# The seams of a four-stage encoder step: what runs at the end of each stage for the next one, and rows of the sample attention every 6 slots

## The chip, the cores and the metric

One core of a Trainium2 chip. The metric is the device time of one execution of the whole kernel in microseconds, here the median of three runs.

## What is computed

One layer of a hybrid encoder on a prompt of 2048 tokens and on 8 sample rows of 16 tokens with 512 cached tokens each, all in float32, d_model 1024:

```python
z = x @ w_in                     # q latent 256 | kv latent 256 | rotary key 32 | pooling 512
q = rms_norm(q_a, g_q) @ w_q_b   # 8 heads x (64 + 32 rotary)
c = rms_norm(c_raw, g_kv); kr = rope(kr_raw)
# prompt: k, v = c @ w_kv_b, softmax over chunks of 64 up to the query's own
# sample: attention in the latent space over cache and new tokens
pool_out = pool_mix(u, windows 2, 4, 8, 16)
mix = concat(attention, pool_out) @ w_o
x1 = layer_norm(ALPHA * x + mix)
x2 = layer_norm(ALPHA * x1 + conv_ffn(x1) + sigmoid(x1 @ w_pg) * (pe @ w_pe))
```

The outputs are x2 for prompt and sample, the latents c, the rotary keys and the states of pooling and convolution.

## The kernel before, in words

Every product of two matrices is made of three matmuls (lines 84 to 86): both operands are split into a high part, rounded to a type that TensorE (PE) takes in one pass, and a low part, the remainder. The high part is written by ScalarE (ACT), the low part by GpSimd (POOL) or VectorE (DVE) as raw minus high. All loads and stores are issued on one queue, SyncE's (SP). Each engine has its program written out in order; semaphores tie them. There are five stages, and at the end of each every engine waits for all others and for the stage's last stores:

- **project** (from 0 to 266.7 us on PE): w_in for 4 chunks of 512 tokens and then for the 128 sample tokens, whose x pieces are loaded and split 512 wide. In the sample's chunk ACT also splits the 8 weight pieces of the next stage (`split_x(HEADS_C, ...)`), between the latents; SP loads them, then stores the pooling state (line 320), the pooled channels (line 284), the latents (line 292) and the rotary key. The third and fourth pool store wait for an earlier one to land. ACT and POOL run the chunks in loops.
- **heads** (282 to 470): PE makes ten idle matmuls (line 1179), then the 8 q units of the sample, then 64 units of six matmuls for the prompt (per chunk 8 of q, 4 of k, 4 of v, in `ORDER`). DVE rotates q units in three operations (lines 998, 1000, 1009), ACT copies the rest (line 883). The 8 rows of the sample attention are spread over these slots: row r starts at slot `ROW_BASE + ROW_PITCH * r` = 5 + 7r, with parts at fixed distances (scores +1, maxima +2, exponents +3, new tokens +4, scaling +4, new low parts +6, transposes +6, values +9, latents +10). `LATENT_AT` is the slot of the latent queries, 2.
- **attend** (475 to 1018): 8 heads, each 4 strips of 512 queries, 320 units of 128 keys. Before a strip's scores its row maxima are found: PE makes the scores once (`peak`, line 1628), DVE reduces them (line 1571), PE turns them into a row (line 1642), ACT writes it into row 96 of the queries (line 1521). PE makes values of unit i - 4 behind the scores of unit i. ACT makes the exponentials (1491) and their high parts (1498), DVE (1600) and POOL (1461) the low parts of even and odd units. When a strip is done ACT copies its sums (`num`, two buffers, line 1541), which go through DRAM twice, and POOL multiplies (line 1441). In the opening DVE clears masks, and row 96 of the keys (1555), and makes the low part of the rotary key's first chunk (1560) ahead of the first maximum. PE starts with 12 idle matmuls (1614). In the last head the first 7 of 18 weight pieces of the next stage and its first tile are split at units given by `MIX_LOW` and `MIX_TILE`, and PE ends with those 7 pieces of tile 0.
- **mix** (1019 to 1463): 17 tiles of 128 tokens: w_o (8 pieces), residual and norm, transposes, w_pe (2 pieces), w_pg (8 pieces, `gates`). At its start pieces 7 to 17, tile 1 and the embeddings are still to be split; a piece waits for its slot in `work`.
- **ffn** (1463 to 3049): not touched.

## Time and profile before

| | us |
|---|---|
| median of 3 runs (3043.7 to 3048.4) | 3046.28 |
| the profiled execution | 3051.59 |
| its span in the profile | 3049.8 |
| PE busy | 2928.4 |
| DVE / ACT / POOL busy | 1632.2 / 1358.0 / 1401.2 |
| share of time that PE's clock was granted in full, as a mean | 0.979 |

"Busy" is the time in which an engine has an instruction running; idle time in front of an instruction is given with what ended it. PEclk is the clock that TensorE was granted, 1.00 being 2.4 GHz and 0.50 being 1.2 GHz; a value between is a mean of the two. Matmuls overlap, so the spacing of their starts is shorter than their duration. Names begin with the stage: pj, hd and sa (sample attention), at, mx, ff; ho is what is handed over between stages.

### The profile page before, as it was taken

Reading aid. Unit: us, or ns where it says so; the run is one execution under the profiler, and the core shown is the slowest. Engines: PE = TensorE matmul, PEld = TensorE weight load, DVE = VectorE, ACT = ScalarE, POOL = GpSimd, SP = SyncE. Lnnn points to the kernel's source line nnn. Section 1 sums busy time; section 2 is a strip of 40 time slices with the busy share of each in tenths; the row PEclk is TensorE's granted clock in tenths of the full one; section 3 lists DMA queues with packets and bytes.
Section 4 is the critical chain, followed back from the end, with each engine's and each line's share of the span. In section 5 each row is a group of like instructions: output and inputs, shape, how many; then the busy total and the mean of one; then the engine's idle time right before and its main releaser. Section 6 shows DMA issues by size and latency. Waiting matters only on the chain.

```text
span 3049.8 us, 43672 instructions
## 1 busy us (share of the span) xinstructions
PE 2928.4 (96%) x15374; PEld 2575.0 (84%) x15374; DVE 1632.2 (54%) x2177; ACT 1358.0 (45%) x2635; POOL 1401.2 (46%) x831
## 2 busy tenths in 40 slices
PE   8996997999999799999999999999999999999997
PEld 6876876777777588888999999999999999999996
DVE  5635787777777444443344343474344447544446
ACT  5343554777777422221434343443333344444443
POOL 5352553676666522222344343574343447544445
PEclk9997997999999899999999999999999999999998
DMA  4226552213223322222421221242121213312221
GB/s 136 87 86 127 164 161 54 42 42 65 42 45 108 117 89 87 89 87 91 174 69 56 68 65 59 92 157 82 49 76 55 69 62 133 123 63 75 76 76 61
DMA packets 161774, 263.67 MB, mean 86 GB/s; under 512 B 48352, under 2 KB 90048, under 8 KB 160288
## 3 DMA queue, kind: packets, MB, share of 16 engines
q1 hardware_dynamic: 161664, 262.27, 28.0%
q8 instruction: 62, 1.02, 0.1%
q14 instruction: 48, 0.39, 0.0%
HBM read 206.34 MB, written 55.88 MB: 86 GB/s over the span
## 4 chain that ended last, share of the span: by engine, by line
PE 51%; DVE 1%; POOL 0%; issue 0%; DVEq 0%; ACTq 0%
PE ff_u L84 11%; PE ff_u L86 11%; PE ff_u L85 11%; PE ff_d L84 5%; PE ff_d L85 5%; PE ff_d L86 5%; DVE ff_y L2552 0%; DVE ff_y L2601 0%; DVE ff_stats L2584 0%; POOL ff_y L2387 0%; POOL ff_rstd L2377 0%; DVEq L2167 0%; DVE ff_mv L2586 0%; DVE ff_neg_mean L2588 0%; POOL ff_offset L2379 0%
## 5 line engine op out<-in xcount | busy, mean ns | idle before, releaser
L2337 POOL TENSOR_TENSOR ff_w_lo<-ho_raw,ff_w_hi 128x1024 fp32r<-128x1024 f32 x99 | 242.6, 2464 | 491.7 <-ACT ff_w_hi L2410 491.7
L2337 POOL TENSOR_TENSOR mx_w_lo<-ho_raw,mx_w_hi 128x1024 fp32r<-128x1024 f32 x97 | 276.0, 2858 | 230.7 <-ACT mx_w_hi L2410 230.7
L2531 DVE SCALAR_TENSOR_TENSOR ff_cv_a<-ff_up_a,ff_taps,ff_cv_a 128x768 f32<-128x768 f32 (+1 forms) x132 | 154.5, 1171 | 347.0 <-ACT ff_cv_a L2459 339.0
L2552 DVE TENSOR_TENSOR ff_y<-ff_y,ff_d 128x512 f32<-128x512 f32 x374 | 239.6, 682 | 146.3 <-PE ff_d L86 146.2
L2531 DVE SCALAR_TENSOR_TENSOR ff_cv_b<-ff_up_b,ff_taps,ff_cv_b 128x768 f32<-128x768 f32 (+1 forms) x132 | 122.7, 930 | 305.4 <-ACT ff_cv_b L2459 296.8
L1461 POOL TENSOR_TENSOR at_p_lo<-at_p,at_p_hi 128x512 fp32r<-128x512 f32 (+2 forms) x160 | 189.7, 1186 | 178.9 <-ACT at_p_hi L1498 177.1
L1600 DVE TENSOR_TENSOR at_p_lo<-at_p,at_p_hi 128x512 fp32r<-128x512 f32 (+1 forms) x160 | 192.3, 1203 | 67.6 <-ACT at_p_hi L1498 67.4
L84 PE MATMUL ff_u<-ho_hi,mx_w_hi 128*128 128x384 f32 (+1 forms) x690 | 224.9, 326 | 0.7 <-ACTq L2403 0.7
L86 PE MATMUL ff_u<-ho_lo,mx_w_hi 128*128 128x384 f32 (+1 forms) x690 | 225.0, 326 | 0.0
L85 PE MATMUL ff_u<-ho_hi,mx_w_lo 128*128 128x384 f32 (+1 forms) x690 | 224.8, 326 | 0.0
L1491 ACT ACTIVATE at_p<-at_s 128x512 f32<-128x512 f32 (+1 forms) x320 | 169.7, 530 | 103.9 <-PE at_s L1664 50.0
L84 PE MATMUL ff_u<-ho_hi,ff_w_hi 128*128 128x384 f32 x630 | 205.1, 326 | 0.0
L86 PE MATMUL ff_u<-ho_lo,ff_w_hi 128*128 128x384 f32 x630 | 205.0, 325 | 0.0
L85 PE MATMUL ff_u<-ho_hi,ff_w_lo 128*128 128x384 f32 x630 | 205.0, 325 | 0.0
L1498 ACT ACTIVATE at_p_hi<-at_p 128x512 fp32r<-128x512 f32 (+1 forms) x320 | 179.2, 560 | 0.0
L2450 ACT ACTIVATE ff_up_b<-ff_u 128x384 f32<-128x384 f32 x110 | 54.0, 491 | 267.6 <-PE ff_u L86 267.6
L84 PE MATMUL ff_d<-ff_w_hi,ff_h_hi 128*128 128x512 f32 x408 | 159.1, 390 | 4.4 <-DVE ff_y L2552 4.4
L2343 POOL TENSOR_TENSOR ff_h_lo<-ff_h,ff_h_hi 128x768 fp32r<-128x768 f32 (+1 forms) x66 | 117.8, 1786 | 91.4 <-ACT ff_h_hi L2470 91.4
L2544 DVE TENSOR_TENSOR ff_h<-ff_cv_a,ff_cv_b 128x768 f32<-128x768 f32 (+1 forms) x66 | 157.6, 2388 | 3.9 <-issue 0.4
L85 PE MATMUL ff_d<-ff_w_hi,ff_h_lo 128*128 128x512 f32 x408 | 159.1, 390 | 0.0
L86 PE MATMUL ff_d<-ff_w_lo,ff_h_hi 128*128 128x512 f32 x408 | 159.0, 390 | 0.0
L2410 ACT ACTIVATE ff_w_hi<-ho_raw 128x1024 fp32r<-128x1024 f32 x99 | 103.4, 1050 | 124.4 <-DMA ho_raw<-in_w_ffn_p 124.4
(471 smaller groups left out, 8858.6 us busy)
## 6 DMA issues: line engine op xcount, KB each, us to landing
ho_raw<-in_w_ffn_p SPq DMA_DIRECT2D x196, 512.0 KB, 3.7
ho_raw<-in_x_t SPq DMA_DIRECT2D x40, 256.0 KB, 3.1
mx_work<-in_w_mix_p SPq DMA_DIRECT2D x18, 512.0 KB, 3.7
ho_raw<-in_x SPq DMA_DIRECT2D x17, 512.0 KB, 4.1
mx_m_raw<-scratch_mix_t SPq DMA_DIRECT2D x17, 512.0 KB, 4.9
scratch_x_t<-mx_work SPq DMA_DIRECT2D x17, 512.0 KB, 3.2
scratch_y<-mx_work SPq DMA_DIRECT2D x17, 512.0 KB, 3.0
ff_y<-scratch_y SPq DMA_DIRECT2D x17, 512.0 KB, 6.2
```

Source lines behind the costliest of these rows:

```text
L84: pe.matmul(out, lh, rh, start=first, stop=False, **kw)
L85: pe.matmul(out, ll, rh, start=False, stop=False, **kw)
L86: return pe.matmul(out, lh, rl, start=False, stop=last, **kw)
L1461: pool.tensor_tensor(p_lo[:, e % H_RING, 0:b - a], p[:, e % P_RING, 0:b - a], f32(p_hi[:, e % H_RING, 0:b - a]), ALU.subtract).then_inc(lo ...
L1491: act.activation(p[:, i % P_RING, 0:b - a], ps_s[i % S_BANKS][:, 0:b - a], ACT.Exp).then_inc(expd, 1)
L1498: act.activation(p_hi[:, i % H_RING, 0:b - a], p[:, i % P_RING, 0:b - a], ACT.Copy).then_inc(hid, 1)
L1600: dve.tensor_tensor(p_lo[:, e % H_RING, 0:b - a], p[:, e % P_RING, 0:b - a], f32(p_hi[:, e % H_RING, 0:b - a]), ALU.subtract).then_inc(lo_ ...
L2337: pool.tensor_tensor(w_lo[slot], w_raw[n % RAWS].rearrange("p (k c) -> p k c", c=P), f32(w_hi[slot]), ALU.subtract).then_inc(wlo, 1)
L2343: pool.tensor_tensor(h_lo[:, i + extra, 0:w], h[:, i, 0:w], f32(h_hi[:, i + extra, 0:w]), ALU.subtract)\
L2531: op = dve.scalar_tensor_tensor(cv[s][:, 0:pw], up[s][:, k:k + pw], tap, cv[s][:, 0:pw], ALU.mult, ALU.add)
L2544: dve.tensor_tensor(h[:, i, 0:w], cv[0][:, 0:w], cv[1][:, 0:w], ALU.mult).then_inc(mul, 1)
L2552: dve.tensor_tensor(y[:, t, H[i]], y[:, t, H[i]], ps_d[2 * (t % 2) + i][:, :], ALU.add)\
```

## The change

- **project** takes the first pair of x buffers from outside, so that heads finds it filled. x of the sample is loaded and split 128 wide, into the second half of the low and high pair's own rows. Head weights 0 to 3 are loaded before the last chunk's latents are stored and split ahead of the sample's pooling; 4 to 7 are split between the sample's pooling units. The first chunk's q latent and kv latent (4 pieces) are loaded behind the state stores and ahead of the pool stores, and split by ACT and DVE. The late stores of pool and latents get own places and semaphores. The loops of POOL and ACT are written out. PE ends with 20 idle matmuls.
- **heads** starts without idle matmuls with the k units of chunk 0; the 8 sample units go in pairs before slots 2 to 5; row r starts at slot 10 + 6r, the latent queries are at slot 7; PE ends with 14 idle matmuls.
- **attend**: PE starts after one memset with 3 idle matmuls, and its maxima wait only for the masks; the ones in row 96 of the keys and the rotary key's first low part are POOL's; `num` has three buffers; pieces and tile of mix at other units; tile 1 and pieces 7, 8 and 9 are split behind the last unit; PE makes all 8 pieces of tile 0, DVE its residual; SP loads pieces 11 to 14.
- **mix** starts with the statistics of tile 0 on DVE and tile 1 on PE; pieces 10 to 17 are left, 15, 17 and 16 loaded here in this order.

```diff
 def project(nc, g, hand, x_pair):
+            def load_first():
+                for i in range(2):
+                    sp.wait_ge(st_lat[i], nth(CHUNKS - 1, 2, 1) * 16)
+                for k in range(4):
+                    sp.wait_ge(split_lo, x_piece(FIRST_C, k) - RAW + 1)
...
-                    if width == SAMPLE and i >= 2:
-                        sp.wait_ge(st_pool[i % 2], nth(c, 2, 0) * 16)
...
-            load_x(SAMPLE_C)
+            load_x(SAMPLE_C, SAMPLE)
...
             store_pool(last, CW)
+            load_head_weights(range(RAW))
             sp.wait_ge(kr_mul, nth(last, 2, 1))
             load_trig(SAMPLE_C)
             store(last, CW)
-            load_head_weights()
+            load_head_weights(range(RAW, KD))
             sp.wait_ge(evac, nth(SAMPLE_C, 8, 3))
             for grp in range(4):
                 sp.dma_start(g["pool_s"][:, grp], rows32(u[:, grp, 0:ROWS * 32])[:, :, 17:32]).then_inc(st_hist, 16)
+            load_first()
             store_pool(SAMPLE_C, SAMPLE)
...
+            def sample_chunk():
+                split_x(HEADS_C, 1, range(RAW))
+                for i in range(4):
+                    keep_u(SAMPLE_C, i, SAMPLE, True)
+                    if i > 0:
+                        difference(SAMPLE_C, i - 1, SAMPLE)
+                        split_x(HEADS_C, 1, (RAW + i - 1,))
+                difference(SAMPLE_C, 3, SAMPLE)
+                split_x(HEADS_C, 1, (KD - 1,))
+                for i in range(4):
+                    if i == 3:
+                        split_x(FIRST_C, 0, (0, 1))
+                    latent(SAMPLE_C, i, SAMPLE)
+                    pooled(SAMPLE_C, i, SAMPLE)
+                split_x(FIRST_C, 0, (2, 3))
+                roots(SAMPLE_C, SAMPLE)
...
+            for _ in range(PJ_TAIL):
+                pe.matmul(ps[0][:, :], w_hi[:, 0, 0, :], w_hi[:, 0, 0:4, :].rearrange("p a b -> p (a b)"), start=True,
+                          stop=True, skip_group_check=True)
...
-HD_WARM = 10
+PJ_TAIL = 20
+HD_TAIL = 14
-UNITS_H = [(CHUNKS, n) for n in range(HEADS)] + [(c, n) for c in range(CHUNKS) for n in ORDER]
+FIRST_ORDER = (8, 9, 10, 11, 0, 12, 1, 13, 2, 14, 3, 15, 4, 5, 6, 7)
+SAMPLES_BEFORE = {2: (0, 1), 3: (2, 3), 4: (4, 5), 5: (6, 7)}
-ROW_PITCH, ROW_BASE, LATENT_AT = 7, 5, 2
-SPLIT_AT = (3, 5, 7, 9)
+ROW_PITCH, ROW_BASE, LATENT_AT = 6, 10, 7
+SPLIT_AT = {c: (8, 9, 10, 11) if c == 0 else (3, 5, 7, 9) for c in range(CHUNKS + 1)}
...
+                if s == 6:
+                    act.wait_ge(uv_in, 16)
+                    act.activation(uv_hi[:], uv_raw, ACT.Copy).then_inc(uvhi, 1)
+                    act.wait_ge(blank, 8)
+                    keys(0)
...
-WARM = 12
+WARM = 3
-MIX_LOW = {283 + 5 * n: n for n in range(7)}
-MIX_TILE = 314
-MIX_FIRST = 7
+MIX_LOW = {285: 0, 287: 1, 293: 2, 297: 3, 305: 4, 307: 5, 309: 6}
+MIX_TILE = 312
+NUM_RING = 3
+MIX_TAIL = NUA
...
             store(STRIPS - 1)
+            sp.dma_start(pre.staged(11), g["w_mix_p"][11]).then_inc(pre.w_in[pre.slot(11)], 16)
+            sp.wait_ge(pre.split_lo, 5)
+            sp.dma_start(pre.staged(12), g["w_mix_p"][12]).then_inc(pre.w_in[pre.slot(12)], 16)
+            sp.wait_ge(pre.wlo_dve, 5)
+            for n in (13, 14):
+                sp.dma_start(pre.staged(n), g["w_mix_p"][n]).then_inc(pre.w_in[pre.slot(n)], 16)
...
+            pool.memset(f32(k_hi[0][96:97, :]), 1.0).then_inc(row_of_ones, 1)
             for s in range(NP_):
                 split(0, s)
+                if s == 1:
+                    pool.wait_ge(kr_hi, 1)
+                    pool.wait_ge(split_lo, 2)
+                    pool.tensor_tensor(k_lo[0][NOPE:96, 0:CW], raw_k[NOPE:96, 0:CW], f32(k_hi[0][NOPE:96, 0:CW]),
+                                       ALU.subtract).then_inc(kr_first, 1)
...
                         act.wait_ge(used, LAST_UNIT[s] + 1)
-                        if s >= 2:
-                            act.wait_ge(normed, s - 1)
+                        if s >= NUM_RING:
+                            act.wait_ge(normed, s - NUM_RING + 1)
...
-            rope_lows(0, 0, 1)
...
-                if i in (-3, 2, 6):
+                if i in (1, 5, 9):
...
+            dve.wait_ge(pre.mixed, 1)
+            dve.wait_ge(pre.x_in[0], 16)
+            dve.wait_ge(pre.wlo_pool, 5)
+            for j in range(2):
+                half = slice(j * CW, (j + 1) * CW)
+                dve.scalar_tensor_tensor(pre.work[:, 0, half], pre.x_raw[:, 0, half], ALPHA, pre.ps_m[j][:, :], ALU.mult,
+                                         ALU.add).then_inc(pre.resid, 1)
...
-            pe.wait_ge(blank, 4)
+            pe.wait_ge(blank, 1)
...
-            pe.wait_ge(cleared, 1)
+            pe.wait_ge(blank, 4)
+            pe.wait_ge(masked, 1)
...
-            for k in range(MIX_FIRST):
+            for k in range(KD):
...
             load_e(0, 0)
-            load_m(1, 1)
+            load_e(1, 1)
             sp.dma_start(ident[:, :], g["ident"]).then_inc(const_in, 16)
-            for n in range(11, len(W)):
+            for n in (15, 17, 16):
                 load_w(n)
...
-            for n in range(7, 11):
-                weight(n)
-            split(0, 0, 1, (1,))
-            split(1, 1, 1)
-            for n in range(11, len(W)):
+            for n in range(10, len(W)):
                 if n == len(W) - 1:
                     act.wait_ge(mixed, at(1, 1, 0))
                 weight(n)
+                if n == 12:
+                    embedding(0, 0, 1)
+                if n == 14:
+                    embedding(1, 1, 1, count=2)
...
-            mix(0, True, range(MIX_FIRST, KD))
             mix(1)
```

## Rows read from the trace of the kernel before

**Rows 1.** The page: span, and busy time of each engine.

```profile
span 3049.8 us, 43672 instructions
...
PE 2928.4 (96%) x15374; PEld 2575.0 (84%) x15374; DVE 1632.2 (54%) x2177; ACT 1358.0 (45%) x2635; POOL 1401.2 (46%) x831
```

**Rows 2.** Waits of PE: who waited for whom, us in total, times, longest.

```profile
PE at_s L1662 <- ACT at_p L1491: 9.1, 8, 1.3
...
PE at_row L1614 <- DVE at_deep L1549: 6.5, 1, 6.5
...
PE sa_s L84 <- DVE sa_n_lo L1013: 3.6, 3, 1.2
PE sa_t L1158 <- DVE sa_prob L1032: 3.5, 3, 1.2
```

**Rows 3.** Busy time by stretch: length, PE, PEld, DVE, ACT, POOL, clock, DMA share, GB/s.

```profile
266.70:282.00 15.30, 0.78 (x4) 0.59 (x3) 4.52 (x11) 0.62 (x2) 0.00 (x0) 0.50 0.62 38
286.00:334.60 48.60, 42.79 (x206) 36.63 (x204) 32.37 (x55) 28.43 (x52) 19.92 (x15) 0.82 0.52 165
334.60:470.00 135.40, 127.24 (x763) 108.63 (x763) 105.35 (x151) 70.26 (x135) 63.81 (x41) 1.00 0.56 170
491.50:501.00 9.50, 8.91 (x33) 7.85 (x31) 8.07 (x19) 6.84 (x12) 3.49 (x3) 0.50 0.53 123
```

**Rows 4.** Timeline and waits of SP and DVE at the end of project.

```profile
259.47 3.20 SPq L320 DMA_DIRECT2D out_pool_s<-pj_u  x4
262.71 13.43 SPq L284 DMA_DIRECT2D scratch_mix_t<-pj_pool_o  x4
...
SPq L283 <- DMA scratch_mix_t<-pj_pool_o: 9.4, 1, 9.4
...
277.93 0.79 DVE L454 SCALAR_TENSOR_TENSOR pj_latn<-ho_raw,pj_gains,pj_rstd 128x128 f32<-128x128 f32 x2 [6.53 <-DMA out_c_t<-pj_latn]
```


**Rows 5.** Timeline of PE in heads; the add ending a rotation (ns, min/median/max), and its busy us, mean ns.

```profile
282.06 4.12 PE L1179 MATMUL hd_ps<-ho_hi 128*128 128x512 f32 x10 [14.58 <-PEq L1283]
...
L1009 DVE TENSOR_TENSOR hd_out<-hd_rot x32: 682/809/2712, 304.5 to 462.8; 32x512 f32<-32x512 f32 x32
...
L1009 DVE TENSOR_TENSOR hd_out<-hd_rot 32x512 f32<-32x512 f32 x32 | 44.8, 1399 | 1.1
```

**Rows 6.** Timeline of POOL, DVE and ACT in the opening of attention.

```profile
476.56 7.42 POOL L1435 TENSOR_TENSOR ho_lo<-ho_raw,ho_hi 64x512 fp32r<-64x512 f32 x6 [23.23 <-ACT ho_hi L1485]
...
479.07 7.57 DVE L1560 TENSOR_TENSOR ho_lo<-ho_raw,ho_hi 32x512 fp32r<-32x512 f32 x1
486.67 0.29 DVE L1571 TENSOR_REDUCE at_neg_max<-mx_m 128x1 f32<-128x128 f32 x1
...
490.40 0.59 ACT L1521 ACTIVATE ho_hi<-at_row 1x512 fp32r<-1x512 f32 x1 [8.52 <-PE at_row L1642]
```

**Rows 7.** Waits of ACT for the numerator buffer in attention.

```profile
ACT at_num L1541 <- POOL at_out L1441: 21.5, 7, 3.1
```

**Rows 8.** Timeline of PE in the last head, waits of over 1.5 us.

```profile
979.46 0.69 PE L1682 MATMUL at_o<-at_p_hi,at_v_one 128*66 128x512 f32 x1 [2.70 <-DVE at_p_lo L1600]
...
1003.72 0.45 PE L1682 MATMUL at_o<-at_p_hi,at_v_one 128*66 128x512 f32 x1 [1.94 <-POOL at_p_lo L1461]
```

**Rows 9.** Timeline of ACT, SP and PE from the last strip to the gates.

```profile
1006.39 0.59 ACT L1541 ACTIVATE at_num<-at_o 65x512 f32<-65x512 f32 x1 [1.85 <-PE at_o L1684]
...
1018.91 0.40 SPq L1804 DMA_DIRECT2D mx_e_raw<-in_pe_t  x1
...
1032.23 0.76 PE L84 MATMUL mx_m<-mx_w_hi,mx_rest_hi 128*128 128x512 f32 x1 [7.88 <-DVE mx_work L1991]
...
1051.44 0.47 PE L84 MATMUL mx_g<-mx_rest_hi,mx_t_hi 128*128 128x512 f32 x1 [2.47 <-DVE mx_t_lo L2015]
1051.75 0.39 PE L85 MATMUL mx_g<-mx_rest_hi,mx_t_lo 128*128 128x512 f32 x1
1051.98 0.40 PE L86 MATMUL mx_g<-mx_rest_lo,mx_t_hi 128*128 128x512 f32 x1
```

More of the change, by code:

```diff
@@ L423, in _ @@
             act.wait_ge(const_in, 32)
-            with act.Fori(0, CHUNKS // 2) as it:
-                chunk(2 * it, 0, CW)
-                chunk(2 * it + 1, 1, CW)
-            chunk(SAMPLE_C, 0, SAMPLE, sample=True)
+            for c in range(CHUNKS):
+                chunk(c, c % 2)
+            sample_chunk()
         @block.vector
@@ L679, in lows, with slot_units, sample, chunk_end @@
         def lows(c, k):
-            if c == 0 and k >= 2:
-                return xlo_dve, k - 1
-            return xlo, 2 + k + 1 if c == 0 else 4 + 4 * (c - 1) + k + 1
+            return xlo, 2 + 4 * (c - 1) + k + 1
+        def slot_units(s):
+            first = sum(len(units) for units in SLOT_UNITS[:s])
+            return range(first, first + len(SLOT_UNITS[s]))
+        def sample(i):
+            return UNITS_H[i][0] == CHUNKS
+        def chunk_end(c):
+            return max(i for i, (d, _) in enumerate(UNITS_H) if d == c) + 1
         def row_at(slot, after):
@@ L839, in _ @@
                 split(CHUNKS, k)
-            for k in range(2):
-                split(0, k)
             pool.wait_ge(blank, 8)
@@ L1208, in _ @@
                 mm.then_inc(valued, 1)
+            for _ in range(HD_TAIL):
+                pe.matmul(ps_n[:, :], hand.hi[:, 0, 0:P], hand.hi[:, 1, :], start=True, stop=True, skip_group_check=True)
 QT = SEQ // P
@@ L1875, in weight, with split @@
                 pool.wait_ge(whi, n + 1)
[L1876 to L1878 removed]
+                pool.tensor_tensor(lo, pre.staged(n), f32(hi), ALU.subtract).then_inc(wlo_pool, 1)
+            def split(t, u, parts=(0, 1), count=1):
                 m_h, m_l = m_pair(t)
@@ L1891, in normalise @@
                     split(*following)
+                if piece is not None:
+                    weight(piece)
                 pool.wait_ge(centred, at(t, 1, 0))
@@ L2060, in _, with mix @@
                 pe.sem_inc(s, 2 * n)
-            def mix(t, first=False, parts=range(KD)):
+            def mix(t, parts=range(KD)):
                 m_h, m_l = m_pair(t)
```

398 lines of the change are left out of this document (229 added, 169 removed).

## The prediction

> **What bounds the kernel now.** I began with the page: TensorE (PE) is busy for 96% of 3049.8 us, the other engines for half [rows 1]. So time goes only where PE waits or where its clock is down, and the 121 us of PE idle (3049.8 - 2928.4) are what a reordering can win. The waits of PE give where: 14.58 us ahead of the heads stage [rows 5], 6.5 ahead of attention and 9.1 inside it [rows 2], 2.70 and 1.94 in its last head [rows 8], 7.88 at the start of mix [rows 9]. The FFN is nearly half of the time and has hardly any. The busy times of chosen stretches then show the clock [rows 3]: it is at 0.50 (1.2 GHz) through 266.7 to 282, down for part of 286 to 334.6 (mean 0.82), and at 0.50 in 491.5 to 501. All of this lies at the four seams that the change touches. I take the seams in order. "Granted" is the mean of two levels, 1.2 and 2.4 GHz.
>
> **1. End of project.** PE's last work ends at 266.7, heads begins at 282.06 [rows 3, 5]. The chain between them is on SP's queue [rows 4]: four stores of the pooling state at 259.47 to 262.7, four pool stores of which the third waits for a landing (9.4 us, and 13.43 for the group), so the latents are stored only behind 276.1, and VectorE (DVE) waits 6.53 us for one of those. The change gives the late stores places and semaphores of their own, so both waits go, some 9 us. It also puts work onto the chain: four first-chunk loads (256 KB each) are issued behind the state stores and ahead of the pool stores; ScalarE (ACT) splits two of them before the last latent and two before the roots, and DVE makes four low parts (0.68 us each, two at the end). State stores need the fourth pooling unit, which now comes some 2 to 3 us later on ACT because ACT waits for head weights 4 to 7 in between, but SP no longer stands behind eight weight loads: I put them at 253.5 instead of 259.5. They drained in about 13.4 us (from 259.5 to 263.5 + 9.4, where the third pool store could go), so the first-chunk data land at 267 to 271. From there: split 0.6 twice, two roots, two reciprocals of 0.95, four scalings, about 5.5 us, store and landing 2, seam 0.9: heads begins at 279. **-3 us** (bounds -7, if the loads overtake the drain, +2, if they land late). The 20 extra matmuls on PE run in this shadow.
>
> **2. Start of heads.** Before, PE issues ten idle matmuls (282.06 to 286.0), then waits 5.8 in all up to 334.6 (48.6 - 42.79), with the clock down for (1 - 0.82)/0.5 = 36% of 48.6 us = 17.5 us, which can cost up to 8.7 [rows 3, 5]. After, the first units' inputs are already split, so PE starts at once: -4.0. Idle -5.8, but the sample's latents are still loaded and split in here (3.7 us until 285.8) behind only two units, and ACT's copies of key parts now stand inside the slots: +3. Clock: PE is idle only some 3 us at the seam instead of 15, so I take half of 8.7: -4.5. **-11.3** (bounds -16: all; -5: the clock stays low and the waits return).
>
> **3. Rows every 6 slots from 10.** The same 64 units and 8 rows; the last row ends in slot 62 instead of 64, so its last low part is hidden: -0.9. Per row DVE has one maximum, sum, scaling and five low parts. Over 334.6 to 470 PE is busy 127.2 of 135.4 and DVE 105.4 [rows 3], so PE has 8.2 us of waits, which in the list come at every second row: 1.2 before the transposes, 1.2 before the next scores (3 of each, 7.1 us) [rows 2]. Those are the rows that start in an odd slot, where the DVE parts fall beside a rotation; with base 10 and pitch 6 all start in even slots. Against that the next scores come one slot (1.5 us) sooner after the DVE part that they need. **-2 with the tail** (bounds -7, all waits gone, +6, 0.8 per row on top).
>
> **4. Start of attention.** This seam is the clearest. DVE starts the first low part of the rotary key at 479.07 and it takes 7.57 us, because POOL runs its six splits from 476.56 to 483.98 and the value split (2.15) behind them without a pause; the other low parts of this form take 0.68. The first maximum is at 486.67, the first exponent row on ACT at 490.40 [rows 6]. In the change that low part is POOL's, the 1.76-us memset of a key row too, and PE starts after one memset with three warm matmuls: the maxima start at 477.3, 9.4 us sooner. The scores follow 4.8 us later, at 482.1. POOL must by then have done the memset (nowhere in the rows; DVE's took 1.76, so 1 to 4), two splits and the key part, 1.24 each: 475.2 + 2 + 3.8 = 481. In time. But POOL's run now lasts to about 475.2 + 2 + 8 x 1.24 + 1.3 + 2.15 = 490.6, and DVE's first two-input operation of the loop (low part of probabilities 0) falls inside it, ready at 486. By the row of 7.57 us a two-input DVE operation starves until the whole run is over: it would end at 491.3 against 497.95 before, -6.7, and everything behind it shifts by that. The Trainium skill, page "SBUF — State Buffer", section "Who interferes with whom", says that the second one to issue is blocked until the first instruction has finished, not until a run has; by it the low part would wait one split, about 1.3 us, and the whole -9.4 would stay. The row speaks for the long wait; I take **-7.5**, nearer to the row (bounds -5, POOL's memset 4 us; -13, all of it and the clock up earlier than 506). The 14 extra matmuls at the end of heads fit into the 6.5 us that PE idles there.
>
> **5. A third numerator buffer.** Once per head ACT waits 3.1 us before the copy of the second strip's sums, because the buffer still waits for POOL's product (7 times, 21.5 us), and right behind it PE waits 1.3 for an exponent [rows 7]. With three buffers the product of the strip needed is 16 or more units older. Cost: 2 KB, nothing on an engine. What is late next is ACT itself, which has slack, 45% busy over the span [rows 1]. **-8.5** (bounds -9.1 and -4).
>
> **6. The mix pieces in the last head.** PE loses 2.70 at 979.46, where DVE starves beside POOL's product, low part and piece 4, and 1.94 at 1003.72, where the low part of the mix tile (2.83) stands on POOL ahead of the probabilities [rows 8]. The change puts piece 4 two units later and the tile two units earlier. **-4** (bounds -6 and +2: piece 6 now shares a step with a product).
>
> **7. Start of mix.** Let E be the end of the last values (1006.35). Before: seven pieces to 1016, the strip's sums go through DRAM twice (copy at E+0.04, the store lands at about E+11.7), mix begins at 1018.9 = E+12.5, the residual of tile 0 ends the wait at 1032.23, gates start at 1051.44 = E+45.1 [rows 9]. After: eight pieces, 48 matmuls of 0.23 (spacing in [rows 9]) = 11.1 us, then the two residuals 1.3: E+12.6, seam to E+13.3, 0.8 later than before; the pieces 7 to 9 and tile 1 are split on ACT and DVE while the sums travel. Mix then starts with tile 1 at once instead of at E+25.9: ends E+24.5. But the gates wait for the pieces: load 16 follows the low part of piece 14 on POOL (S+13, S being mix's start), lands S+17, and ACT takes pieces 16 and 17, 1.06 each, before it copies the turned tile, table load 1.28, two copies, low part 0.69: gates at S+22.4 = E+35.7. **-10** (bounds -16, if the pieces are no limit; -5).
>
> **Sum.** -3 - 11.3 - 2 - 7.5 - 8.5 - 4 - 10 = -46.3. The profiled execution took 3051.59 (span 3049.8), 5.3 above the median of 3046.28; it would take 3005, and the median becomes **3000 us**. The FFN is untouched, the project loops written out add no PE work. PE runs 15 idle matmuls more in all (10 + 9 out, 20 + 14 in), all inside seams where it would idle.
>
> **Rivals.** (a) *The seams give back a part.* The clock falls anyway in the thinner stretches (PE is ready for work but fed by ACT and DVE) and the first-chunk loads land late: terms 1, 2, 4, 7 at -0, -6, -5, -5, the rest as summed: -30, 3016. For it: the clock stayed at 0.50 for 16 us in attention's opening although PE was busy for 94% of 491.5 to 501. Against: half of 286 to 334.6 ran at the upper level in spite of 5.8 us of waits. Chance 0.14. (b) *More goes than summed.* Clock up across three seams, pieces no limit: -6, -15, -5, -11, -9, -5, -16 = -67, 2979. Chance 0.10. (c) *The change does not do what it says*: the ring of three moves ACT's wait to another strip and the reordered pieces keep their stalls: +12.5 on the sum, 3012; inside the range, part of the forecast. (d) *Slower: DVE starves in heads.* The add that ends a rotation takes 0.68 alone and up to 2.71 beside POOL; its mean is 1.40 in 32 [rows 5]. Rows at pitch 6 put the same POOL work into fewer slots. If all 32 took 2.7, that is 42 us of DVE; it has 30 free in the 135 of [rows 3], and the ones that stand before a wait of PE would delay it directly. It becomes the bound from a mean of about 2.3. To reach slower it would also have to hold the probabilities' low parts in attention's first head (20 on DVE at 2.5 instead of 1.2, +26): 42 - 30 + 26 + about 20 of direct delays = +58 on -46, 3058. Against: the mean work per row is the same as now. Chance 0.03.
>
> **How the numbers follow.** The forecast as summed, with its errors partly cancelling (2986 to 3014), has 0.70; (a) 0.14, (b) 0.10, (d) 0.03, and 0.03 for a small net effect from mishaps that I don't see. The range 2978 to 3020 takes in the forecast and most of (a) and (b). What a measurement of this kernel tells from no change is 0.2%, 6 us. Faster by more than that: 0.95; within: 0.02; slower: 0.03.
>
> **What would show it.** Right: heads' first matmul near 279 and on real units; in the first 50 us of heads a granted clock above 0.9; the first maximum about 2 us after attention's first memset; no wait of the numerator copy on POOL's product; gates of tile 0 some 36 us after the last values. Wrong: a wait of ACT for first-chunk loads longer than 8 us, DVE's rotation adds above a mean of 2, a wait of PE before row scores above 2 us per row, probabilities' low parts of 5 us behind POOL's opening splits, or gates that still start 45 us behind the values.

## The result and the profile after

The changed kernel takes **3022.53 us** (median of 4 runs, 3021.11 to 3022.98) against 3047.34 (4 runs, 3043.7 to 3050.38) for the kernel before: a ratio of 0.9916, 95% interval 0.9904 to 0.9929, so 0.8% faster. I had forecast 3000, range 2978 to 3020. The direction was right; of 46 us, 25 came by the medians and 28.7 by the two profiled executions (span 3021.1 against 3049.8). Run again beside the experiments, the kernel before has medians of 3048.99 to 3050.74, so by the medians the gain lies between 25 and 28.

The page of the changed kernel, span and PE's line, to be read beside [rows 1]:

```profile
span 3021.1 us, 43561 instructions
...
PE 2938.2 (97%) x15389; PEld 2586.1 (86%) x15389; DVE 1618.7 (54%) x2178; ACT 1352.3 (45%) x2632; POOL 1393.3 (46%) x830
```

PE's idle time is 82.9 us instead of 121.4, a gain of 38.5; but PE is busy for 9.8 us longer, with work that is the same but for the idle matmuls. Those take 11.1 us in all instead of 8.1, so 3.0 of the 9.8 is theirs. In the other 6.8 the same matmuls take longer; whether by the clock or otherwise I did not take apart.

I laid five marks into each timeline: the first matmul of heads, the end of heads' last product, the first score of attention, the end of the last values, the first gate of tile 0. All in us from the start of the span; later kernels of this study are in the same table.

| kernel | heads begins | heads' last product | first score | last values end | first gate | span |
|---|---|---|---|---|---|---|
| before | 282.06 | 469.96 | 491.52 | 1006.35 | 1051.44 | 3049.8 |
| changed | 280.98 | 465.22 | 478.02 | 981.47 | 1021.53 | 3021.1 |
| e1_stores_first | 282.19 | 460.10 | 472.91 | 976.24 | 1016.52 | 3017.5 |
| e2_keys_later | 281.96 | 463.12 | 475.94 | 978.24 | 1019.28 | 3019.4 |
| e3_gates_first | 280.91 | 462.97 | 476.46 | 979.10 | 1014.40 | 3014.9 |
| e4_two_num | 280.67 | 461.81 | 474.62 | 985.61 | 1025.83 | 3026.4 |
| e5_no_tails | 283.22 | 464.91 | 477.72 | 978.95 | 1019.58 | 3019.6 |
| e6_before_rows6 | 281.92 | 463.51 | 485.10 | 997.93 | 1043.46 | 3041.8 |
| e7_keep_first | 282.18 | 464.80 | 477.34 | 979.55 | 1020.59 | 3021.7 |
| e8_all_four | 280.27 | 459.78 | 472.49 | 977.19 | 1013.80 | 3014.1 |
| e9_first_last | 280.51 | 464.85 | 477.69 | 979.38 | 1020.21 | 3019.9 |
| e10_row0 | 282.06 | 457.93 | 470.49 | 972.51 | 1006.80 | 3004.4 |
| e11_all | 279.86 | 457.40 | 469.96 | 973.22 | 1006.60 | 3007.0 |
| e12_before_low | 281.17 | 469.80 | 491.37 | 1000.12 | 1045.89 | 3045.6 |
| e13_both_chains | 277.39 | 456.82 | 469.63 | 970.91 | 1004.04 | 3004.0 |

The table also shows how much one execution of the same code varies: heads takes 184.2, 182.1, 181.1, 182.6 and 184.3 us in the five kernels that leave it as changed (changed, e3, e4, e7, e9), mean 182.9; before 187.9 and 188.6 (before, e12). So a difference of 2 us in heads between two single profiles says nothing. From the first gate to the end every kernel takes 1997.6 to 2001.1.

By stages the gain is: heads begins 0.4 earlier (mean 281.3 of the changed kernel, e1 to e4, e8 and e10, against 281.7 of before, e6 and e12), heads 5.4 shorter (188.3, the mean of before and e12, against 182.9), from its end to the first score 8.8 (21.56 to 12.80), attention 11.4 in the profiled execution (514.83 to 503.45), from the last values to the gates 5.0 (45.1 to 40.1). These add up to 31.0; up to the first gate the profiled execution of the changed kernel has 29.9 of it and behind the gate it is 1.2 longer. The forecast for the five was 3, 13.3, 7.5, 12.5 and 10.

PE's waits in heads in the changed kernel, the list of who waited for whom between 281 and 466 (total us, times, longest):

```profile
PE hd_ps L84 <- ACT hd_out L958: 4.1, 1, 4.1
PE sa_n L1200 <- issue: 3.7, 1, 3.7
PE sa_n L1200 <- ACT sa_prob L995: 2.0, 1, 2.0
...
PE hd_ps L84 <- POOL ho_x_lo L889: 1.7, 1, 1.7
PE sa_s L84 <- DVE sa_n_lo L1085: 0.8, 2, 0.6
```

The six waits of 1.2 at every second row ([rows 2], 7.1 us) are gone, as forecast. But a wait for an output copy (4.1) and two longer ones before the new-token transposes (3.7 and 2.0) stand in their place, so that all waits inside the stage come to 12.3 us against 13.9 before. And the clock is no better: the stretches of the changed kernel to 330 and on to 341 (columns as in [rows 3]):

```profile
281.00:330.00 49.00, 42.01 (x204) 35.07 (x204) 29.87 (x55) 23.30 (x43) 16.85 (x14) 0.86 0.58 183
330.00:341.00 11.00, 7.92 (x27) 5.99 (x28) 9.94 (x12) 6.04 (x12) 5.16 (x3) 0.69 0.23 60
```

It is 0.86 where [rows 3] had 0.82, but during the wait of 3.7 it falls to 1.2 GHz once more (331 to 338), in a stretch where the kernel before ran at 2.4. Worked out from these rows, the clock is down for 13.7 + 6.8 = 20.5 us up to 341, against 17.5 in [rows 3]. That is where the missing part of the forecast starts.

### The profile page after: what moved, and what is told of

Read it like the earlier page. It is cut to its first block, busy times and chain, and to the rows that moved or that the text cites. A ratio compares the mean times of both kernels' runs of the same rounds, so it can differ in the third digit from the quotient of the medians.

```text
span 3021.1 us, 43561 instructions
## 1 busy us (share of the span) xinstructions
PE 2938.2 (97%) x15389; PEld 2586.1 (86%) x15389; DVE 1618.7 (54%) x2178; ACT 1352.3 (45%) x2632; POOL 1393.3 (46%) x830
## 4 chain that ended last, share of the span: by engine, by line
PE 51%; DVE 1%; POOL 0%; issue 0%; DVEq 0%; ACTq 0%
PE ff_u L84 12%; PE ff_u L86 12%; PE ff_u L85 11%; PE ff_d L84 6%; PE ff_d L85 6%; PE ff_d L86 6%; DVE ff_y L2682 0%; DVE ff_y L2731 0%; DVE ff_stats L2714 0%; POOL ff_y L2517 0%; POOL ff_rstd L2507 0%; DVEq L2297 0%; DVE ff_mv L2716 0%; DVE ff_neg_mean L2718 0%; POOL ff_offset L2509 0%
```

## The experiments

### 1. The first key stores behind the value loads

What holds ACT and then PE for 4 us? The timelines of SP, ACT and PE in the changed kernel:

```profile
295.17 0.80 SPq L832 DMA_DIRECT2D sa_v_raw<-in_ckv  x2
296.03 2.84 SPq L807 DMA_DIRECT2D scratch_k_t<-hd_out  x4
...
302.04 0.59 ACT L958 ACTIVATE hd_out<-hd_ps 64x512 f32<-64x512 f32 x1 [7.53 <-DMA scratch_k_t<-hd_out]
...
302.68 0.50 PE L84 MATMUL hd_ps<-ho_x_hi,ho_hi 128*128 128x512 f32 x1 [4.09 <-ACT hd_out L958]
```

The first four units of heads are now key units. Their copies fill the four output buffers by 293.5, but SyncE stands in front of the value loads until the low part of `w_uk` is made (3.9 us, until 295.2), and only then issues the first store. It lands at 302. In the kernel before eight sample units came first, which are not stored at all.

```diff
+FIRST_STORES = 3
...
-            load_values(0)
-            load_values(1)
             for s in range(SLOTS):
                 if s > 0:
                     store(OWN[s - 1])
+                if s == FIRST_STORES:
+                    load_values(0)
+                    load_values(1)
```

> The changed kernel with one edit: in heads SyncE issues the stores of the first two key units before the two loads of cached values, not behind them. In the changed kernel ACT waits 7.5 us for the first key store (issued at 296.0, landed at 302.0) and PE 4.09 us at 302.68 behind it. Theory (the store ring is held by SyncE's order: stores stand behind loads that wait for a low part): the wait of 4.09 goes, and the clock that fell right after it (0.66 in 310 to 320) stays up longer; heads ends 4 to 8 us earlier, the whole is 3015 to 3019. Rival (the DMA engines are full until 302 anyway, share 0.9 to 1.0, so an earlier store lands as late): at most 1 us, 3022.

Measured: 3018.75 (3017.47 to 3021.27), 3.8 below the changed kernel; heads takes 177.9, 5.0 less than the mean of 182.9. ACT's wait is down to 3.8 and PE's to 0.4, and the granted clock from 282 to 342 is 0.89 (the changed kernel 0.83 from 281 to 342). The theory holds. The rival has a part: the first store is issued at 292.6 instead of 296.0 and, with the DMA engines full (share 1.09 in 291 to 299.6), lands at 299.6 instead of 302.

### 2. The key splits ahead of the exponents

With a pitch of 7, ACT split the keys of the next row 3 slots after a row's start, behind that row's exponents. The distance stayed 4 slots ahead of the next row, so with a pitch of 6 the split falls one slot ahead of the exponents.

```diff
-                r = row_at(s, -4)      # on ACT and on POOL, the same edit twice
+                r = row_at(s, -3)
```

> The changed kernel with the key and query splits of a sample row on ACT and POOL one slot later, that is behind the exponents of the row before as in the kernel before (there 3 slots after a row's start, in the changed kernel 2, because the pitch went from 7 to 6 and the distance stayed at 4). Theory (ACT stands in line with a key split that waits 2.6 us for its load, and the exponents behind it are late): the PE waits of 3.67 at 332.5 and 2.02 at 384.5 shrink to under 1.5 together, ACT waits no longer for key loads, heads ends 3 to 6 us earlier, 3017 to 3020. Rival (the key low parts now come late for the next scores): waits ahead of the scores grow by 0.5 us per row, heads ends 2 to 4 us later, 3025.

Measured: 3025.47 (3021.14 to 3027.1), no gain; in the profile heads takes 181.2. The waits of 3.7 and 2.0 did go (1.1 is left of them), and ACT waits for no key load, so the theory names them rightly. But a single new wait took their place, neither what the theory nor quite what the rival said (it comes once, not per row). PE's waits and DVE's timeline around 335:

```profile
PE sa_s L84 <- DVE sa_n_lo L1085: 5.1, 1, 5.1
```

```profile
331.68 1.92 DVE L1081 TENSOR_TENSOR hd_out<-hd_rot 32x512 f32<-32x512 f32 x1
333.71 0.69 DVE L1070 SCALAR_TENSOR_TENSOR hd_rot<-hd_ps,hd_trig 32x512 f32<-32x512 f32 x1
334.43 0.70 DVE L1072 SCALAR_TENSOR_TENSOR hd_rot<-hd_ps,hd_trig 32x512 f32<-32x512 f32 x1
335.16 2.57 DVE L1081 TENSOR_TENSOR hd_out<-hd_rot 32x512 f32<-32x512 f32 x1
337.76 0.41 DVE L1085 TENSOR_TENSOR sa_n_lo<-sa_n,sa_n_hi 16x256 fp32r<-16x256 f32 x1
```

The changed order of chunk 0 ends in five q units in a row (units 4 to 7 and the next chunk's first), each 2.1 us or more of DVE against 1.4 of PE, and POOL's key and value low parts now run beside them (the adds take 1.92 and 2.57 instead of 0.68). The small low part that row 1's scores wait for stands behind them.

### 3. The gates behind pieces 16 and 17

ACT, POOL and PE of the changed kernel at mix's start:

```profile
1004.11 3.30 POOL L2023 TENSOR_TENSOR mx_work<-mx_work,ho_raw 128x1024 f32<-128x1024 f32 x1 [0.63 <-DVE mx_work L2137]
1007.38 1.70 POOL L2012 TENSOR_TENSOR mx_e_lo<-mx_e_raw,mx_e_hi 128x256 fp32r<-128x256 f32 x1
1009.04 3.34 POOL L2004 TENSOR_TENSOR mx_rest_lo<-mx_work,mx_rest_hi 128x1024 fp32r<-128x1024 f32 x1
...
1015.80 1.06 ACT L2051 ACTIVATE mx_rest_hi<-mx_work 128x1024 fp32r<-128x1024 f32 x1 [12.37 <-DMA mx_work<-in_w_mix_p]
1016.77 1.04 ACT L2051 ACTIVATE mx_odd_q_lo<-mx_work 128x1024 fp32r<-128x1024 f32 x1
1017.82 1.28 ACT L2076 ACT_TABLE_LOAD   x1
1019.12 0.60 ACT L2076 ACTIVATE mx_work<-mx_t 128x512 f32<-128x512 f32 x1
...
1021.53 0.77 PE L84 MATMUL mx_g<-mx_rest_hi,mx_t_hi 128*128 128x512 f32 x1 [5.83 <-DVE mx_t_lo L2148]
```

```diff
-            for n in range(10, len(W)):         # ACT
+            for n in range(10, len(W) - 2):
...
+            step(0, 0, 2, pieces=(16, 17))      # copies of tile 0, then the pieces
+            step(1, 1, 2)
-            with act.Fori(0, 7) as it:
+            with act.Fori(1, 7) as it:
...
-            weight(17)                          # DVE
+            step(0, 0, 1, 17)                   # low part of tile 0, then the piece
```

> The changed kernel with the first step of mix written out: ACT copies the turned tile 0 before it splits pieces 16 and 17, DVE makes the tile's low part before piece 17's. Theory (PE's 5.83 us ahead of the first gates are ACT's queue: pieces 16 and 17 stand ahead of the copies and 16 waits 12.4 us for its load): the wait goes, gates start at the end of the embedding product, some 34.5 us behind the last values instead of 40.1; 5 to 6 us less, 3017. Rival (the pieces themselves are the limit, PE then waits inside the gates for piece 16 or 17): 2 us less, and a wait of 3 to 4 us inside the gates.

Measured: 3016.39 (3014.84 to 3017.2), 6.1 less. The gates start 35.3 behind the last values instead of 40.1, and the wait of 5.83 is gone; a later wait of 1.5 (the next tile's low part) stands in its place. The theory holds: it was the order on ACT, with 12.4 us of standing for a load.

### 4. Two numerator buffers again

```diff
-NUM_RING = 3
+NUM_RING = 2
```

> The changed kernel with two numerator buffers again. The start of the copies, strip by strip, says that the third buffer is worth 1.61 us per head, seven times, 11.3. If so: 3034, with ACT waiting about 21 us for POOL's products and PE 1.6 us per head behind it. By the sum before the result: 8.5, 3031. Rival (with the other seams moved, the ring no longer matters): under 2 us.

Measured: 3033.0 (3028.17 to 3035.66), 10.5 more, and in the waits of ACT the line of [rows 7] is back:

```profile
ACT at_num L1650 <- POOL at_out L1533: 20.5, 7, 3.1
```

From the first score to the last values it takes 511.0 against 502.6, the mean of the eleven kernels with three buffers (501.2 to 504.7): 8.4. Strip by strip the start of the copies slips by 1.6 or 1.7 per head for six heads (9.7 in all). In the last head the wait costs nothing: from the copy of strip 28 to the end of the values this kernel takes 48.2, that of run 3, with three buffers, 48.4. Both sizes are close to the forecast's 8.5.

### 5. Without the idle matmuls at the seams

```diff
-PJ_TAIL = 20
-HD_TAIL = 14
+PJ_TAIL = 0
+HD_TAIL = 0
```

> The changed kernel without the 20 idle matmuls at project's end and the 14 at heads' end. Theory A (they keep the clock up over the two seams): the clock of the first 10 us of heads falls from 0.83 to 0.5 and of 462 to 472 from 1.0 to below 0.8; heads takes 2 to 3 us more, attention's first scores 1 to 2 us more: 3026. Theory B (the clock falls anyway within the next stage, since PE waits 3 to 4 us at three places in heads and works thinly in attention's opening): under 1.5 us in all, 3022 to 3024, the low stretches only move.

Measured: 3021.57 (3021.41 to 3024.76), the same as with them. Stretches of the kernel without them, then of the changed kernel:

```profile
281.00:291.00 10.00, 7.78 (x28) 6.52 (x29) 4.25 (x12) 2.24 (x6) 0.87 (x2) 0.58 0.56 144
291.00:301.00 10.00, 9.16 (x58) 7.81 (x56) 7.88 (x18) 3.85 (x7) 0.00 (x0) 1.00 0.94 308
301.00:321.00 20.00, 16.40 (x70) 13.99 (x71) 6.36 (x12) 9.06 (x15) 6.14 (x3) 0.66 0.33 116
461.00:471.00 10.00, 3.91 (x53) 3.54 (x51) 2.48 (x5) 2.90 (x6) 0.88 (x1) 0.79 0.26 72
```

```profile
281.00:291.00 10.00, 8.32 (x40) 6.91 (x40) 5.13 (x15) 2.89 (x8) 0.87 (x2) 0.83 0.68 195
...
301.00:321.00 20.00, 18.32 (x82) 15.56 (x83) 10.88 (x15) 12.04 (x22) 8.57 (x6) 0.74 0.27 95
461.00:471.00 10.00, 7.50 (x68) 6.26 (x66) 2.49 (x4) 2.94 (x5) 0.58 (x1) 1.00 0.26 73
```

The idle matmuls do lift the clock next to them (0.58 to 0.83, 0.79 to 1.00). It buys nothing in the times: 3021.57 against 3022.53. From 301 to 321 the clock is low either way (0.66 and 0.74). Heads begins at 283.22 here, later than in any other kernel, but takes 181.7, and ends within the spread of the others. Theory B holds.

### 6. Rows every 6 slots alone, in the kernel before

```diff
-ROW_PITCH, ROW_BASE, LATENT_AT = 7, 5, 2
+ROW_PITCH, ROW_BASE, LATENT_AT = 6, 10, 2
-        LAST_SLOT = ROW_BASE + ROW_PITCH * (ROWS - 1) + 11
+        LAST_SLOT = max(SLOTS, ROW_BASE + ROW_PITCH * (ROWS - 1) + 11)
```

> The kernel before with one part of the change alone: the rows of the sample attention start at slot 10 + 6r instead of 5 + 7r, in its own order of units. The forecast's term for this was -2 (from -7 to +6). Theory (the pitch puts the key splits of the next row ahead of the exponents of this one on ACT, and ACT stands there for a load): PE waits of 1 to 4 us before the new-token transposes of two or three rows take the place of the 7.1 us of waits of 1.2, heads changes by -1 to +2, the whole 3045 to 3050. Rival (rows in even slots are free of waits, and what stalled the changed kernel is its order of the first units): -4 to -7, 3041.

Measured: 3045.51 (10 runs, 3043.6 to 3051.51) against 3050.74, ratio 0.9987, 95% interval 0.9977 to 0.9996; in the profile heads takes 181.6 instead of 187.9 and 188.6, so 6.7 less. PE's waits between 286 and 463:

```profile
PE sa_n L1130 <- issue: 3.7, 1, 3.7
PE sa_n L1130 <- ACT sa_prob L920: 1.9, 1, 1.9
PE hd_ps L84 <- DVE hd_rot L1000: 1.6, 1, 1.6
```

Both sides were partly right: the two waits at the new-token transposes are the pitch's (the kernel before has only 1.6 there), but the six waits of 1.2 and others are gone, 7.2 in all instead of 13.9. So rows every 6 slots are worth 6.7 us in the profile and 4.0 by the ratio (its interval: 1 to 7), and the rest of the change in heads, its new beginning, is worth nothing: with both, heads takes 182.9 instead of the 181.6 here. The waits of 3.7 and 1.9 stand at the same rows as in the changed kernel, so they come with the pitch, not with the new beginning.

### 7. The pooling unit before the head weights

```diff
             def sample_chunk():                # ACT
-                split_x(HEADS_C, 1, range(RAW))
                 for i in range(4):
                     keep_u(SAMPLE_C, i, SAMPLE, True)
+                    if i == 0:
+                        split_x(HEADS_C, 1, range(RAW))
...
-            store(last, CW)                    # SyncE
-            load_head_weights(range(RAW, KD))
+            store(last, CW, range(RAW, KD))    # the loads between the two pairs of stores
```

> The changed kernel, project's end: ACT copies the first pooling unit of the sample before it splits head weights 0 to 3 (now behind them, PE waits 0.74 us at 243.2), and SyncE loads weights 4 to 7 between the two pairs of latent stores instead of behind them (ACT waits 2.4 us for weight 4, PE 1.5 at 252.9). Theory (these waits delay PE and with it the pooling chain, and the clock falls to 0.5 behind the first of them, at 246): the clock stays at 1.0 to about 255, heads' first matmul comes 4 to 8 us earlier than 281, 3015 to 3019. Rival (the clock falls there anyway, PE being fed by single products): heads starts 1 to 2 us earlier, 3021.

Measured: 3021.97, no change; heads begins at 282.18. The wait of 0.74 is gone and the clock stayed at 2.4 GHz until 251 instead of 246, not until 255: PE now waits 2.71 us for ACT's copy of a pooling unit, up to 251.55, and works at 1.2 GHz behind it. So the theory's first half holds in part, and its second half falls. ACT now stands for the first chunk's data:

```profile
270.66 0.63 ACT L399 ACTIVATE ho_x_hi<-ho_raw 128x512 fp32r<-128x512 f32 x1 [4.95 <-DMA ho_raw<-scratch_qn_t]
```

### 8. Four edits together

```diff
+FIRST_ORDER = (8, 9, 10, 0, 11, 1, 12, 2, 13, 3, 14, 4, 15, 5, 6, 7)
+                r = 1 if s == ROW_BASE + ROW_PITCH - 4 else row_at(s, -3) if s > ROW_BASE + ROW_PITCH else None
```

and the edits of 1 and 3.

> The changed kernel with four edits together: the first key stores ahead of the value loads (-3.8 alone by the times), mix's turned tile copied before pieces 16 and 17 (-6 alone), the key and query splits one slot later from row 2 on only (row 1 keeps its slot, where the later split cost a wait of 5.1), and the q units of chunk 0 alternating from the fourth slot on instead of four in a row at its end. Theory (DVE's rotations, 2.1 us per q unit against 1.4 of PE, bunch at the end of chunk 0, just where row 0 has its exponents and scaling): the waits of 3.7 and 2.0 ahead of the new-token transposes fall under 2 together and the clock stays up in 330 to 350; heads ends 6 to 9 us earlier than in the changed kernel, in all 3008 to 3011. Rival (row 0's stall is ACT's, table load and splits, whatever DVE does): the wait of 3.7 stays, 3012 to 3014.

Measured: 3014.52 (3011.38 to 3015.88). The wait of 3.7 stays to the tenth, the one of 2.0 is gone, heads takes 179.5. The rival is right for row 0: its stall stays although DVE's units are spread. On ACT two key splits (1.09, 0.64), a value split (1.06) and the table load (1.28) stand ahead of row 0's exponents.

### 9. The first chunk's pieces last

```diff
-                    if i == 3:                 # ACT
-                        split_x(FIRST_C, 0, (0, 1))
                     latent(SAMPLE_C, i, SAMPLE)
                     pooled(SAMPLE_C, i, SAMPLE)
-                split_x(FIRST_C, 0, (2, 3))
                 roots(SAMPLE_C, SAMPLE)
+                split_x(FIRST_C, 0, range(4))
...
-                    first_lows((0, 1))     # DVE, ahead of the rotary key
-                    first_lows((2, 3))     # DVE, at the end
+                    first_lows(range(4))   # DVE, at the end
```

> The changed kernel, project's end: ACT splits the four pieces of the first chunk behind the last latent, the last pooling unit and both roots, and DVE makes their low parts last, where now two pieces stand ahead of the last latent and two ahead of the roots. In the changed kernel the pieces' data land at about 270 and the last latents are stored 5 to 8 us behind. Theory (the pieces hold the latents up on ACT): the last latents are stored at 273 to 275 instead of 277.3, heads starts at 277.5 to 279 instead of 281; 3019. Rival (heads then waits for the split pieces instead, or the latents' stores queue behind the same transfers): heads starts at 280.5 to 281.5, no change.

Measured: 3020.85, heads begins at 280.51: the rival's place, but not by its cause. The pieces are out of the way, yet DVE, and the roots behind it, wait for PE's unit of the rotary key, which PE makes at 1.2 GHz:

```profile
271.61 0.28 DVE L565 TENSOR_TENSOR pj_kr_t<-pj_pool,pj_trig 32x128 f32<-32x128 f32 x1 [13.19 <-PE pj_pool L86]
```

### 10 and 11. Row 0's queue on ACT

```diff
+FIRST_ORDER = (8, 0, 9, 1, 10, 2, 11, 3, 12, 4, 13, 5, 14, 6, 15, 7)
+            act.activation(early_exp[:, :], raw[:, 4, 0:1], ACT.Exp)    # ahead of the slots
```

with the edits of 1, 2 and 3 (e10_row0), and with that of 9 too (e11_all).

> The changed kernel with the first key stores ahead of the value loads, mix's turned tile copied before pieces 16 and 17, the key and query splits one slot later for all rows, units of chunk 0 strictly alternating between k or v and q, and one tiny exponential of ACT at the start of heads, so that the load of its table (1.28 us, now between the value split and the exponents of row 0) is done by then. Theory (row 0's stall of 3.7 is ACT's queue: key split 1.09 and 0.64, value split 1.06, table 1.28 ahead of the exponents; the 5.1 that came for it was DVE's bunched q units): no wait of over 1.5 us left in 320 to 400, heads from its first matmul to its end in 175 to 178 us (the changed kernel 184, with the stores and other edits 179.5), 3009 to 3012. Rival (DVE's adds starve beside POOL's run of row 1 whatever the order): the 3 to 5 us stay ahead of the scores of row 1, 3014.

> Both of the two kernels above in one. If both theories hold: heads starts at 278 and takes 175 to 178, 3006 to 3009. If the first fails, as the second alone.

Measured: 3008.66 (3006.21 to 3012.16) and 3006.81 (3005.99 to 3008.79). In the first heads takes 175.9, and of PE's waits between 286 and 460 these are left:

```profile
PE hd_ps L84 <- DVE hd_rot L1076: 2.8, 2, 2.6
PE sa_s L84 <- DVE sa_n_lo L1089: 2.5, 2, 1.6
PE hd_ps L84 <- POOL ho_x_lo L892: 2.5, 1, 2.5
PE sa_s L84 <- DVE sa_pt_lo L1146: 0.3, 1, 0.3
```

No wait at a new-token transpose is left, and the largest one of row 1 is 1.6. The theory holds: with ACT's queue for row 0 shortened and DVE's q units spread both stalls are gone, where 2 and 8 each removed only a part. What the order of the units and the early table load (now at 286.75) do by themselves, no run shows. The second kernel begins heads at 279.86, neither at the 278 of its expectation nor at the 282.06 of the first.

One low stretch of the clock stays in the first kernel as it was in the changed one, and in both PE is busy without a gap (the changed kernel, then e10_row0):

```profile
311.00:321.00 10.00, 10.00 (x39) 8.63 (x39) 3.06 (x4) 4.65 (x10) 5.06 (x5) 0.68 0.16 52
```

```profile
311.00:321.00 10.00, 10.00 (x43) 8.61 (x43) 2.32 (x3) 4.83 (x9) 6.65 (x6) 0.66 0.14 48
```

So not every fall of the clock in heads comes from a wait of PE.

### 12. The mix pieces alone, in the kernel before

```diff
-MIX_LOW = {283 + 5 * n: n for n in range(7)}
-MIX_TILE = 314
+MIX_LOW = {285: 0, 287: 1, 293: 2, 297: 3, 305: 4, 307: 5, 309: 6}
+MIX_TILE = 312
```

> The kernel before with one part of the change alone: the first seven pieces and the first tile of mix split at the changed units of the last head (pieces from 285 in uneven steps instead of 283 + 5n, tile at 312 instead of 314). The forecast's term for this was -4 (-6 to +2). In the profiles the last head, from the copy of strip 28 to the end of the values, takes 52.6 us before and 50.3 or 48.4 in executions of the changed code. Theory: the waits of 2.70 at 979.5 and 1.94 at 1003.7 go, the last head takes 48.5 to 49.5; 3 to 4 us less than before. Rival (the third numerator buffer does that): 52 to 52.5, no change.

Measured: the last head takes 48.2 (951.95 to 1000.12) instead of 52.6, and its waits of 2.70 and 1.94 [rows 8] are gone: 4.4, the theory. The times, 3047.18 (10 runs) against 3048.99, ratio 0.9995, 0.9985 to 1.0005, fit a gain of 4.4 and none at all, so the size rests on the profiles.

### 13. Both chains at the end of project

e11_all with the edits of 7.

> The kernel with all six edits (e11_all) and the two edits of e7_keep_first in project. Alone, the earlier pooling unit and weights left heads at 282.2, because ACT then stood for the first-chunk pieces until their data landed at 270.7; alone, the pieces behind the roots left it at 280.5, because PE, at 1.2 GHz since 244, ended the unit of the rotary key only at 271.6. Theory (two chains end within 1 us of each other, and only both together move the start): with both, the last latents are stored at 274 to 275, heads starts at 277 to 278.5, 1.5 to 3 us before e11_all; 3004 to 3005.5. Rival (a third limit, the stores and transfers themselves): heads starts at 279.5 to 280.5 as in e11_all.

Measured: **3005.17** (3002.1 to 3006.42). The last latents and the first matmul of heads:

```profile
271.53 0.81 SPq L315 DMA_DIRECT2D out_c_t<-pj_latn  x2
273.70 0.81 SPq L315 DMA_DIRECT2D scratch_qn_t<-pj_latn  x2
...
277.39 0.48 PE L84 MATMUL hd_ps<-ho_x_hi,ho_hi 128*128 128x512 f32 x1 [2.65 <-PEq L1368]
```

The theory holds: each edit alone moved the start by under 1 us, within the 280.3 to 282.2 of the kernels without either, both together by 3.9 from their mean of 281.3. Little of it reaches the end of heads: against e11_all the start is 2.5 earlier and the end 0.6, because heads takes 179.4 instead of 177.5 in this execution, and the ranges of the times overlap. This kernel beats both: ratio to before 0.9855 (0.9838 to 0.9871), 17 us below the changed one.

## Why the prediction was wrong

**1, end of project: -0.4 instead of -3.** The waits on stores went as said, and the first two pieces of the first chunk landed at 269.5 and 270.1 (issue and time to landing), inside the 267 to 271 of the forecast. But I costed the rest of the chain from there at 5.5 us to the last store; it takes 7.1 (split at 270.21, query latents stored at 277.29), because the second root on ACT stands behind DVE's first reciprocal and its scalings. From that store to heads it takes 3.7, not 2.9. And I looked at one chain only. PE's, at 1.2 GHz since 246, ends within a microsecond of it (runs 7, 9 and 13); in the changed kernel itself the profile puts ACT's wait of 3.1 ahead of the first split to PE's last unit, the rotary key's, which frees the pieces' place. "The 20 extra matmuls run in this shadow" was right.

**2, start of heads: about 0 instead of -11.3, the step that failed.** Its bounds were -16 and -5. Rows every 6 slots alone bring heads to 181.6 us (run 6), this new beginning with them to 182.9. Of its parts, the idle matmuls gone, -4.0, is right. Idle -5.8 + 3 was wrong in sign: this stretch (to 330) has 7.0 us without PE work where the one of [rows 3] had 5.8. I followed PE's inputs and not the outputs: four stored units now come first, they fill the output buffers, and SyncE stands at a load ahead of the first store (run 1: 4 to 5 us). The clock at -4.5 was wrong too: it is down for 20.5 us instead of 17.5. It falls at 304, one microsecond behind the wait of 4.09, at 311, where PE is busy without a gap, and at 331, inside the wait of 3.67; idle matmuls before the seam change only the first ten microseconds (run 5). The last piece, the q units bunched at the end of chunk 0 beside row 0, wasn't seen at all (runs 2, 8, 10).

**3, rows every 6 slots: -6.7 by the profile of run 6 and -4.0 by the ratio of its times, instead of -2,** inside the bounds of -7 and +6. The even slots did away with the waits of every second row, as argued. What I had missed is a distance kept at 4 slots when the pitch shrank: the key splits passed the exponents on ACT (waits of 3.7 and 1.9).

**4, start of attention: -8.8 against -7.5.** The maxima start 2.55 us after the first memset, and scores 4.9 later (forecast 4.8). My reason for taking less than -9.4 was wrong. POOL, then DVE in the changed kernel:

```profile
476.31 4.99 POOL L1527 TENSOR_TENSOR ho_lo<-ho_raw,ho_hi 64x512 fp32r<-64x512 f32 x4
481.26 2.17 POOL L1527 TENSOR_TENSOR at_v_lo<-at_raw_v,at_v_one 128x1024 fp32r<-128x1024 f32 x1
483.40 2.95 POOL L1527 TENSOR_TENSOR ho_lo<-ho_raw,ho_hi 64x512 fp32r<-64x512 f32 x2
486.31 1.44 POOL L1564 TENSOR_TENSOR at_p_lo<-at_p,at_p_hi 128x384 fp32r<-128x384 f32 x1
...
483.89 1.33 DVE L1668 TENSOR_TENSOR ho_lo<-ho_raw,ho_hi 32x512 fp32r<-32x512 f32 x1
485.25 1.65 DVE L1706 TENSOR_TENSOR at_p_lo<-at_p,at_p_hi 128x512 fp32r<-128x512 f32 x1
```

POOL runs without a pause, and DVE's two-input operations take 1.33 and 1.65 us instead of 0.68: they get in behind one instruction, not behind the run. That is what the Trainium skill says (page "SBUF — State Buffer", section "Who interferes with whom"), and this trace agrees with it; the 7.57 us of [rows 6] beside the same kind of run remain an exception that no run here explains. The first low part of the probabilities still ended only 6.3 us earlier relative to the memset, near the 6.7 that I had reckoned for the wrong reason. ACT has no part in that: its high part is done 5.4 us behind the first score in both kernels (483.44 and 496.93). It is the two operations shown, which take 2.98 together where before one of 0.68 stood there. From the first score to the first strip's copy it takes 22.6 us instead of 21.0, so about 1.6 of the 8.8 is lost again, and that -7.5 came close is in part luck.

**5 and 6, attention: -11.4 against -12.5.** Each was near its size: 8.4 for the third buffer (run 4; forecast 8.5), 4.4 for the pieces (run 12; forecast 4). Together they come to 12.8; the stage has 11.4. In the changed kernel the copies of heads 1 to 7 give 10.6, the last head 2.3 and the opening takes the 1.6 back. In the last head the profiled execution of the changed kernel is 1.8 us slower than e3 (50.2 from strip 28 to the end, e3 48.4), of which no run shows the cause.

**7, start of mix: -5.0 instead of -10.** Mix begins at E+13.8 by its first matmul, E+13.1 by its first load (forecast 13.3), and the copies behind pieces 16 and 17 were named as the limit. Only their load was put too early: at S+13 and landing at S+17, in truth at S+17.1 and S+20.6, because it waits for POOL, where the product, the embedding's low part and piece 14's took 3.30, 1.70 and 3.34 beside DVE. The low part of the same form at 1001.05 took 2.42. Run 3 shows that the order on ACT decides: there piece 16 is split no sooner (22.0 us behind mix's start), and yet the gates start at E+35.3.

The rivals: (a) was the nearest (the seams give back a part, 3016, 0.14), with the right terms at fault, 1, 2 and 7 (its fourth, the start of attention, was not), but mostly through queues, less through the clock. (b) did not come: neither the clock nor the pieces gave more than summed. (c) is refuted: the ring gives 8.4 (run 4) and the moved pieces lose their stalls (run 12). (d) is refuted: the adds of the rotation have a mean of 0.93 us in the changed kernel, 1.40 before [rows 5]. Of the signs that I had named for a wrong forecast none came; the two that count, a wait for an output buffer and one before the new-token transposes, were not among them.

## What to carry to other kernels

When the units at the start of a stage are put in another order, follow what they leave behind as well as what they need: the output buffers, the store queue and what stands ahead of the first store in it. Offsets written as distances to the next step must be gone through again when the pitch changes. And a seam that two chains reach within a microsecond shows nothing when one of them is shortened; look at both before costing either.

## What was not expected of the hardware

- Idle matmuls ahead of a seam raise the granted clock of the following 10 us from 0.58 to 0.83 and change the time by less than a run varies (3021.57 against 3022.53).
- A wait can cost twice: behind the one of 4.09 us that ends at 302.68 the matmuls run at 2.4 GHz for one microsecond, then at 1.2 until 307. In the one of 3.67 that ends at 332.5 the clock falls before PE starts again (0.69 in 330 to 341).
- The clock also falls where PE doesn't wait: 0.68 in 311 to 321 with PE busy for all 10 us, and 0.66 in the same stretch of e10_row0.
- The same code in the same place varies by 3 us in heads (181.1 to 184.3) and by 2 in the last head, more than several of the terms argued about here.
